# High weights times both halves of the input in one matmul, in 40 of 88 first-layer tiles

## The reference, cut to what matters

```
even mixer   : z = norm(x) @ w_in; gates, short convolution, pooling; @ w_out
gated FFN 0  : z = norm(x) @ w_in; (silu(conv(u)) * g) @ w_out
odd mixer    : z = norm(x) @ w_in -> q, k, v; two kinds of attention, 16 heads; @ w_out
gated FFN 1  : as FFN 0; final norm
latent attention (mla), conditioned by ada_w and ada_b
squared-ReLU MLP 0:  square(relu(modulate(x) @ w1)) @ w2         w1: 1024 x 4096, w2: 4096 x 1024
gated mixer  : z = gelu(modulate(x) @ w_in); u, v = halves;
               v = layernorm(v); mixed = ws @ v + bs (per group);  (u * mixed) @ w_out   u: 2048 wide
squared-ReLU MLP 1:  as MLP 0
```

## Time and profile before

| | us |
|---|---|
| median of 3 runs (lowest, highest) | 1261.15 (1259.61, 1263.08) |
| the profiled execution's own time | 1261.2 |
| its span, first to last instruction | 1259.5 |
| TensorE, VectorE, ScalarE busy | 1239.7, 952.3, 649.0 |
| f tiles' matmuls: 1408 of each of three kinds | mean 284 ns each, overlapping |

### The profile page before, as it was taken

How to read it: one execution, slowest core, us unless ns; L and a number is a source line. 1 busy time by engine, 2 the same in 40 slices (tenths; PEclk the granted TensorE clock), 3 DMA queues, 4 the chain that set the end, 5 groups by cost and what they waited for, 6 DMA issues and landing times.

```text
span 1259.5 us, 20228 instructions
## 1 busy us (share of the span) xinstructions
PE 1239.7 (98%) x7959; PEld 1114.2 (88%) x7959; DVE 952.3 (76%) x1185; ACT 649.0 (52%) x972; POOL 125.8 (10%) x237
## 2 busy tenths in 40 slices
PE   6999999999999999999999999999999999999998
PEld 5989999989867999999899879999888998899987
DVE  4867888967685888898788787998675888666644
ACT  5555454546465654445677565444463353643441
POOL 3000000000010121110132300120010010000000
PEclk9999999999999999999999999999999999999999
DMA  9656777655462698993222347998556487386540
GB/s 330 206 167 199 237 244 249 240 167 173 162 219 68 201 324 309 321 334 125 70 74 99 134 137 271 392 392 281 179 175 227 168 299 269 104 307 209 197 134 34
DMA packets 151600, 265.27 MB, mean 211 GB/s; under 512 B 5915, under 2 KB 108037, under 8 KB 151533
## 3 DMA queue, kind: packets, MB, share of 16 engines
q1 hardware_dynamic: 134544, 204.75, 48.6%
q0 software_dynamic: 16544, 59.07, 13.1%
q10 hardware_dynamic: 445, 0.53, 0.1%
HBM read 263.26 MB, written 1.06 MB: 210 GB/s over the span
## 4 chain that ended last, share of the span: by engine, by line
PE 88%; DVE 7%; ACT 2%; issue 1%; POOL 1%; DMA 0%; ACTq 0%; POOLq 0%; DVEq 0%
PE ps L1824 24%; PE ps L1805 13%; PE ps L1807 13%; PE ps L1806 13%; DVE w_lo L1086 2%; PE ps L1867 2%; PE ps L1869 2%; PE ps L1868 2%; PE ps L1845 2%; PE ps L1847 2%; PE ps L1846 2%; PE ps L1929 2%; PE ps L1931 2%; PE ps L1930 2%; PE ps L2138 1%
## 5 line engine op out<-in xcount | busy, mean ns | idle before, releaser
L1086 DVE TENSOR_TENSOR w_lo<-raw,w_hi 128x2048 fp32r<-128x2048 f32 (+3 forms) x213 | 437.9, 2069 | 106.7 <-ACT w_hi L563 106.4
L563 ACT ACTIVATE w_hi<-raw 128x2048 fp32r<-128x2048 f32 (+3 forms) x213 | 369.4, 1739 | 139.9 <-PE ps L1824 102.4
L1805 PE MATMUL ps<-xn_hi,w_hi 128*128 128x256 f32 x1408 | 400.5, 284 | 0.0
L1807 PE MATMUL ps<-xn_hi,w_lo 128*128 128x256 f32 x1408 | 399.1, 283 | 0.0
L1806 PE MATMUL ps<-xn_lo,w_hi 128*128 128x256 f32 x1408 | 399.1, 283 | 0.0
L1805 PEld LDWEIGHTS ps<-xn_hi,w_hi 128*128 128x128 f32 x1408 | 270.8, 192 | 2.7 <-issue 0.7
L1806 PEld LDWEIGHTS ps<-xn_lo,w_hi 128*128 128x128 f32 x1408 | 270.7, 192 | 2.4 <-issue 0.5
L1807 PEld LDWEIGHTS ps<-xn_hi,w_lo 128*128 128x128 f32 x1408 | 270.7, 192 | 0.0
L1824 PE MATMUL ps<-w_hi,a_hi 128*128 128x512 f32 x432 | 134.6, 393 | 0.2 <-DVE a_lo L1746 0.2
L1824 PE MATMUL ps<-w_lo,a_hi 128*128 128x512 f32 x432 | 133.5, 390 | 0.0
L1824 PE MATMUL ps<-w_hi,a_lo 128*128 128x512 f32 x432 | 133.2, 390 | 0.0
(11 more groups left out here) (336 smaller groups left out, 1762.0 us busy)
## 6 DMA issues: line engine op xcount, KB each, us to landing
raw<-in_ffn_w SPq DMA_DIRECT2D x64, 1024.0 KB, 5.7
side<-in_ada_w POOLq DMA_DIRECT2D x96, 512.0 KB, 6.4
raw<-in_ffn_w_in SPq DMA_DIRECT2D x40, 1024.0 KB, 5.6
raw<-in_ffn_w_out SPq DMA_DIRECT2D x32, 512.0 KB, 6.2
raw<-in_gm_w_in SPq DMA_DIRECT2D x16, 1024.0 KB, 5.9
raw<-in_od_w_in SPq DMA_DIRECT2D x12, 1024.0 KB, 5.3
raw<-in_ev_w_in SPq DMA_DIRECT2D x8, 1024.0 KB, 11.1
raw<-in_gm_w_out SPq DMA_DIRECT2D x8, 1024.0 KB, 5.5
```

Source lines behind the costliest of these rows:

```text
L563: nc.scalar.activation(w_hi[s][:, 0:w], raw[s][:, 0:w], ACT.Copy).then_inc(hi_done, 1)
L1086: nc.vector.tensor_tensor(w_lo[s][:, 0:w], raw[s][:, 0:w], w_hi[s][:, 0:w].bitcast(F32), ALU.subtract)\
L1805: nc.tensor.matmul(o, hi, xn_hi3[:, k, :], start=k == 0, stop=False)
L1807: last = nc.tensor.matmul(o, lo, xn_hi3[:, k, :], start=False, stop=k == KB - 1)
```

## The change

Of the 88 f tiles, 40 are made by `f_wide`: attention input tiles 2 to 7, steps 2 to 15 of both squared-ReLU MLPs, steps 0 to 5 of the gated mixer. `xn_hi` and `xn_lo` become two halves of one tensor, and one matmul multiplies high weights with both side by side (512 columns, in two pieces), filling a bank: the high half's product in columns 0 to 255, the low half's in 256 to 511. The low weights' product is added to the first half. So there are two matmuls (512 and 256 columns) in place of three of 256, and a tile fills two banks, one for each block of features. ScalarE copies the low halves of both banks to SBUF (`low_copy`), VectorE adds the high halves to them (`join`), and only then does ScalarE apply scale, ReLU or GELU, from SBUF. In the squared-ReLU MLPs ScalarE also squares, VectorE no longer does, and VectorE's split of tile f+4 comes after `a_lo`.

```diff
-        xn_hi, xn_lo = sb("xn_hi", [P, KB * S], F32R), sb("xn_lo", [P, KB * S], F32R)
+        xn = sb("xn", [P, 2 * KB * S], F32R)
+        xn_hi, xn_lo = xn[:, 0:KB * S], xn[:, KB * S:]
+        xn_both = xn[:, :].rearrange("p (c k t) -> p k c t", c=2, k=KB)
...
+        def wide(bank):
+            v = banks[:, 512 * bank:512 * bank + 1024].rearrange("p (b c t) -> p b c t", b=2, c=2)
+            return v[:, :, 0, :], v[:, :, 1, :]
...
+        GM_WIDE = 6
+        J_QK, J_RELU0 = 0, 6
+        J_GM = J_RELU0 + R_STEPS - 2
+        J_RELU1 = J_GM + GM_WIDE
...
+            def low_copy(dst, bank):
+                nc.scalar.activation(pair(dst), wide(bank)[1], ACT.Copy).then_inc(low_out, 1)
...
+            def join(x, bank, count):
+                dve.wait_ge(low_out, val(count))
+                nc.vector.tensor_tensor(pair(x), wide(bank)[0], pair(x), ALU.add).then_inc(join_done, 1)
...
+            def f_wide(t, bank, mid=None):
+                t = t if isinstance(t, Aff) else Aff(t)
+                pe.wait_ge(lo_done, val(t + 1))
+                for b in range(2):
+                    o = ps[bank + b]
+                    if b and mid is not None:
+                        mid()
+                    for k in range(KB):
+                        hi, lo = parts(t.c % SLOTS, k * 256 + b * P, P)
+                        nc.tensor.matmul(o[:, :].rearrange("p (c t) -> p c t", c=2), hi, xn_both[:, k], start=k == 0, stop=False)
+                        last = nc.tensor.matmul(o[:, 0:S], lo, xn_hi3[:, k, :], start=False, stop=k == KB - 1)
+                last.then_inc(w_used, 1)
```

ScalarE and VectorE in a step of a squared-ReLU MLP:

```diff
                     else:
                         act.wait_ge(w_used, val(f + 1))
-                    nc.scalar.activation(r_r, ps[bank][:, :], ACT.Relu).then_inc(g["relu"], 1)
-                    if j.c >= 2:
+                        low_copy(r_r, 2 * par)
                         split(f + 4)
-                    act.wait_ge(g["sq"], val(j + 1))
+                        act.wait_ge(join_done, val(j + (joins - 1)))
+                        src = r_r
+                    nc.scalar.activation(r_r, src, ACT.Relu).then_inc(g["sq"], 1)
+                    act.wait_ge(g["sq"], val(j * 2 + 1))
+                    nc.scalar.activation(r_s[par], r_r, ACT.Square).then_inc(g["sq"], 1)
+                    act.wait_ge(g["sq"], val(j * 2 + 2))
...
-                    dve.wait_ge(g["relu"], val(j + 1))
-                    nc.vector.tensor_tensor(r_s[par], r_r, r_r, ALU.mult).then_inc(g["sq"], 1)
                     if j.c >= 2:
-                        split(f + 4)
+                        join(r_r, 2 * par, j + (joins - 1))
...
+                    for unit, slot in units[:2]:
+                        ada(unit, slot, kb)
                     dve.wait_ge(g["ahi"], val(j + 1))
                     c = slice(a_slot(j, par) * 512, a_slot(j, par) * 512 + 512)
                     nc.vector.tensor_tensor(a_lo[:, c], r_s[par], a_hi[:, c].bitcast(F32), ALU.subtract).then_inc(g["a_ready"], 1)
...
+                    split(f + 4)
+                    for unit, slot in units[2:]:
+                        ada(unit, slot, kb)
```

The gated mixer, ScalarE, VectorE, TensorE:

```diff
             def gm_step(j):
                 f, par = T_GM + f_at(j, GM_STEPS), j % 2
-                act.wait_ge(w_used, f + 1)
-                nc.scalar.activation(gm_u, ps[par][:, :], ACT.Gelu).then_inc(GM["u"], 1)
+                if j < GM_WIDE:
+                    act.wait_ge(w_used, f + 1)
+                    low_copy(gm_u[par], 6 if j == 1 else 0)
+                    act.wait_ge(join_done, J_GM + j + 1)
+                else:
+                    act.wait_ge(w_used, f + 1)
+                nc.scalar.activation(gm_u[par], gm_u[par] if j < GM_WIDE else ps[par][:, :], ACT.Gelu).then_inc(GM["u"], 1)
                 if 2 <= j < GM_STEPS - 1:
                     split(f + 4)
...
                 f, par = T_GM + f_at(j, GM_STEPS), j % 2
+                if 2 <= j < GM_WIDE:
+                    gm_join(j)
                 dve.wait_ge(GM["m_ps"], j + 1)
...
             gm_slice(0)
             split(T_GM + 2)
+            gm_join(0)
             split(T_GM + 3)
             dve.wait_ge(GM["bs_in"], 16)
             gm_step(0)
+            gm_join(1)
             gm_norm(1)
...
             def gm_u(j):
                 if j >= 2:
-                    pe.wait_ge(GM["u"], j - 1)
-                f_tile(T_GM + f_at(j, GM_STEPS), j % 2)
+                    pe.wait_ge(join_done, J_GM + (1 if j == 2 else min(j, GM_WIDE)))
+                if j < GM_WIDE:
+                    f_wide(T_GM + f_at(j, GM_STEPS), 6 if j == 1 else 0)
+                else:
+                    f_tile(T_GM + f_at(j, GM_STEPS), j % 2)
...
             gm_mix(1)
+            pe.wait_ge(join_done, J_GM + 2)
             gm_t_step(0)
```

More of the change, by code:

```diff
@@ L121, in build @@
         rel = sb("rel", [33, 8])
-        ps = [ctx.enter_context(nc.psum_tensor(f"ps{i}", [P, 512], F32)) for i in range(8)]
+        banks = ctx.enter_context(nc.psum_tensor("ps", [P, 8 * 512], F32))
+        ps = [banks[:, 512 * i:512 * i + 512] for i in range(8)]
         ident = cst[:, C_ID:C_ID + P]
@@ L363, in build @@
         FFN = [group(f"ffn{n}", "a0", "tap", "conv", "silu", "prod", "ahi", "a_ready") for n in range(2)]
-        RELU = [group(f"relu{n}", "relu", "sq", "ahi", "a_ready") for n in range(2)]
+        RELU = [group(f"relu{n}", "sq", "ahi", "a_ready") for n in range(2)]
         AT = group("at", "qk", "v_sb", "v_act", "z_ps", "z", "nabs", "ez", "ln", "neg", "f_ps", "f", "sel", "s_ps", "s_sb",
@@ L1002, in _ @@
                 split(T_GMV + 2 * c + 5)
-            gm_u = wk(6144, 512)
+            gm_u = [wk(6144 + 512 * m, 512) for m in range(2)]
             gm_t = [acc[:, 4, 512 * m:512 * m + 512] for m in range(2)]
@@ L1384, in _, with at_join @@
             split(T_QK + 5)
+            def at_join(j):
+                join(wk(512 * j, 512), 2 * (j % 2), J_QK + j - 1)
+            at_join(2)
             dve.wait_ge(in_small, 16 * 5)
@@ L1632, in relu0_mods @@
                 dve.wait_ge(ada_ps, 6)
-                shift_cols(16, ps[3][:, 0:8], 1, 0)
-                shift_cols(32, ps[3][:, 16:24], 1, 3)
-                gain_cols(24, ps[3][:, 8:16], 1, 1, g_mix1).then_inc(mod_ready, 1)
+                shift_cols(16, ps[0][:, 0:8], 1, 0)
+                shift_cols(32, ps[0][:, 16:24], 1, 3)
+                gain_cols(24, ps[0][:, 8:16], 1, 1, g_mix1).then_inc(mod_ready, 1)
             def relu(n, base):
-                g = RELU[n]
+                g, joins = RELU[n], J_RELU1 if n else J_RELU0
                 def step(j, par, f, more, kb=None):
-                    dve.wait_ge(g["relu"], val(j + 1))
-                    nc.vector.tensor_tensor(r_s[par], r_r, r_r, ALU.mult).then_inc(g["sq"], 1)
                     if j.c >= 2:
-                        split(f + 4)
+                        join(r_r, 2 * par, j + (joins - 1))
+                    units = []
+                    if kb is not None:
+                        units = [(kb * 4 + (U_RELU0 + c), c) for c in range(4)] if n == 0 else [(kb + U_RELU1, 1)]
+                    if n == 1 and kb is not None and kb.c:
+                        dve.wait_ge(side_used, val(kb + U_RELU1))
+                    for unit, slot in units[:2]:
+                        ada(unit, slot, kb)
                     dve.wait_ge(g["ahi"], val(j + 1))
@@ L1671, in relu @@
                         gate_rows(1 if n else 2, (2, 3), U_BC3 if n else U_BC2)
-                    if n == 0 and j == 14:
-                        relu0_mods()
+                if n == 0:
+                    relu0_mods()
             relu(0, T_RELU0)
@@ L1757, in gm_step, with gm_join @@
                     split(f + 5 + m)
+            def gm_join(j):
+                join(gm_u[j % 2], 6 if j == 1 else 0, J_GM + j + 1)
             gm_slice(0)
             split(T_GM + 2)
+            gm_join(0)
             split(T_GM + 3)
```

96 lines of the change are left out of this document (54 added, 42 removed).

## The result

The changed kernel takes 1266.88 us (median of 5 runs, 1265.74 to 1268.95), the kernel before 1261.27 beside it (1259.61 to 1263.08). The ratio is 1.0044, 95% interval [1.0029, 1.0059]: slower by 5.6 us. The prediction was 1263.2, with 1267 as the upper end of its range. The profiled execution took 1265.74, span 1263.9, which is 4.4 over the span of before.

What follows compares the result with a forecast made beforehand. The prediction took TensorE, busy 98% of the span, as the bound. Attention -0.9, squared-ReLU layers -3.0 each, relu0's end +0.1 and mixer +8.8 summed to +2.0 us, hence 1263.2 us; range 1258.5 to 1267.

Steps and rivals of the forecast that it cites:

- +2.0 us: Whole kernel: predicted net change, the sum of all stage terms, taking the time to 1263.2 us.
- The squared-ReLU layers: Both squared-ReLU MLPs: 14 wide tiles each save 0.213 us a tile, 3.0 us a layer, -6.0 together.
- 0.227 for the wide: TensorE in wide tiles: 0.227 us between starts of 512-column products, beside 0.120 for narrow ones, 0.347 a pair.
- nothing, if a wide product followed by a narrow one hides its weight load worse: Wide tiles on TensorE: lower bound of the saving, none at all, where 0.213 us a tile was taken.
- End of relu0, +0.1: End of the first squared-ReLU layer: conditioning sums moved behind the last step cost 0.1 us.
- Attention, -0.9: Attention input's six wide tiles: TensorE saves 1.3 us, the last join delays some; -0.9 taken, bounds 0 to -1.3.
- Mixer, +8.8: Gated mixer's six wide tiles: joins make TensorE wait; +8.8 us, own 1.3 of savings included, bounds -1.3 to +11.
- The walk: Gated mixer, three engines timed instruction by instruction: tile 4 idles TensorE 3.55 us, tail +6.5, residual +8.95.
- Transfers bind in relu0: First squared-ReLU layer: seven steps loading conditioning weights stay at 11.22 us, 1.5 us lost, 1264.7; chance 0.12.
- Joins hidden: Mixer: VectorE's idle stretches take the six joins, 8.5 us come through less 0.4 in attention, 1253; chance 0.10.
- The wide product is no cheaper: Wide tiles: a two-piece product at 0.24 us instead of 0.227 removes the -6.9 saving, 1270; chance 0.04.
- The clock's case: After the mixer's new idle the clock falls; up to +1.5 us at the boundary, as much next, 1264.7 to 1266.2; chance 0.20.

Runs made afterwards that it cites:

- x3: Changed kernel with each block of a wide tile reordered, all eight wide products first, then the eight narrow ones; 1267.25 us, ratio 1.0043.
- x1: Changed kernel with the mixer's six wide tiles made narrow again, leaving 34 wide tiles; 1257.95 us, ratio 0.9966.
- x5: Changed kernel with a narrow mixer and, in its 34 wide tiles, eight wide products then eight narrow ones per block; 1255.67 us, ratio 0.9955.
- x4: Kernel before with only the mixer's six wide tiles and their joins added; 1271.72 us, ratio 1.0078.
- x9: Changed kernel with only the mixer's first two tiles wide, the third tile's first product waiting for the first join alone; 1258.20 us, ratio 0.9970.
- x3 again: Second set of runs of the same kernel as x3; median 1265.39 us, ratio 1.0031.
- x2: Changed kernel with ScalarE's split in the mixer moved ahead of its wait for the join; 1260.77 us, ratio 0.9991.
- x6: Changed kernel with ScalarE's mixer split ahead of its join wait, and eight wide then eight narrow products per block; 1259.90 us, ratio 0.9989.

## Why the prediction came out as it did

The mechanism was right: the layers gain, the mixer loses more, through TensorE's waits for joins. The forecast was 3.7 us low. That the time lies inside the range, by 0.1 us, is in part luck: the forecast gives the kernel +2.0 us and it lost 5.6, and 1266.9 is beyond the 1264.9 above which the prediction put slower, at a chance of 0.32 against 0.57 for the same. The +2.0 is a small difference of large terms, and three of the terms were off to the same side. By its own steps:

- **The squared-ReLU layers, -6.0: the mis-sized term.** Measured -1.6 each (14 tiles at 0.113; the rest of relu0's -1.9 is the moved `fold_out`). The step that failed is "0.227 for the wide" beside 0.120 for the narrow: both starts were read among equal neighbours, and in turn the pair costs 0.353 and not 0.347. The bound "nothing, if a wide product followed by a narrow one hides its weight load worse" was the side to look at, and x3 shows that it is the taking in turn: grouped, the same 32 matmuls take 5.56 us a tile and the step 11.03, against the 11.01 of the forecast. What makes the change cost some 6 ns a pair, no run shows: the two kinds differ in width and in the pieces of their moving operand (two for the wide one, one for the narrow), and both change at each step. (The 0.347 of the prediction would by itself give 0.208 a tile, not 0.213.)
- The Trainium skill (TensorE: Matmul & The Clock Gate, Back-to-back issue gap) gives its fixed part of 2.5 ns for an isolated matmul; by it, as an estimate, the 34 wide tiles of x1 would save 1.4 us. The median gives them 3.5, and 5.7 in x5 with its grouped order. These rows do not agree with the 2.5: once the neighbours are equal, about the 13 ns of the earlier trace rows stand (0.119 and 0.229 in x3).
- **End of relu0, +0.1**: measured 0.0. Relu0 took 0.40 more than relu1 before and takes nothing more now, but the 0.4 come back at the head of the mixer's stretch (x1).
- **Attention, -0.9**: -0.5 at an equal clock (x1). The joins hide, as said; the tiles save half.
- **Mixer, +8.8**: +9.2, by x1 and by x4; the 9.5 of the table hold the moved `fold_out` too. The walk had tile 4 behind an idle of 3.55 (row: 3.37), the tail at +6.5 and the residual at +8.95. With the mixer's first tile starting 3.2 us earlier than in before (970.12 for 973.33), these are 1063.1 and 1070.4; the rows have 1063.50 and 1070.73. The boundary's transposes waited 2.20, as read.
- **Transfers bind in relu0** (1264.7): no; steps are 11.11 at share 1.05. **Joins hidden** (1253): no, by x1 and x4 together; but x9 shows it true of the first two. **The wide product is no cheaper** (1270): no, but the pair gives back half of what it should save.
- **The clock's case**: it fell at tile 4, as it was feared, and was covered there: tile 4 took 7.28 us for some 5.65 and yet TensorE waited again, 0.53 and then 2.20 at the boundary. The median is 1.1 us over the profiled run. In the other four runs the mean clock was 0.995 to 0.997 for 0.999, and a fall at the attention costs 1.3 to 3.2 us in the traces that have one. That those four runs fell there is likely, not shown, since they left no rows.

In sum: 2.8 us too much from the layers, 0.4 too little for the mixer, 0.4 in the attention at an equal clock, and 0.1 back at relu0's end: 3.5 of the distance of 3.7 from 1263.2 to 1266.9.

## What to carry to other kernels

Before putting a second engine's operation between TensorE and the engine that reads PSUM, walk the ring of waits one time round: a join of 0.7 us cost 2.2 us a tile where TensorE, ScalarE and VectorE wait for each other in turn and each tile writes the banks of the last, and 0.2 a tile where neither was so. Put on each engine what others wait for, and what needs no wait, ahead of the engine's own wait; moving one split a step won back 6.1 us, more than all forty wide tiles save (40 x 0.113). Price a mixed sequence of matmuls by rows of that mixture, and try equal ones side by side.

## What of the hardware was not expected

- Matmuls of 512 and 256 columns, each with its own weights, take 0.353 us a pair in turn and 0.3475 grouped by eight.
- The granted clock is not a property of the kernel. At the same 3.6 us of eight-column products and behind them it stayed at 1.00 (after, x3), fell for some 3.5 us (before, x1) or for 6 to 7 (x3 again, x9): 71.6 to 74.9 us for one stretch. Around an idle of 2.0 us on TensorE it fell in x2 and not in x6; around the idle of 3.3 to 3.4 us in the wide mixer it fell in all four traces that have one (after, x4, and both of x3). The kernel before too has runs at three levels, 1259.9, 1261.4 and 1263.0, with mean clocks of 1.000, 0.999 and 0.997.
- The stretch up to 261 us varies by 1.5 us between executions (260.06 to 261.53), ahead of anything that the change touches. All of it is there within the first 33 us: TensorE's first matmul, which waits for a transfer, starts at 8.99 in x2 and at 10.17 in x1, and the tiles that start at 31.43 and 32.88 already lie 1.45 apart.
